# Two transformer blocks at 256 tokens: the first 33 blocks of modulation products moved from DVE to PE

## The reference

```
s_lat, s_ctx = silu(c), silu(c_ctx)
for l in range(2):
    mod   = s_lat @ w_ada[l] + b_ada[l]      # 1024 -> 6 * 1024
    mod_c = s_ctx @ w_ada[l] + b_ada[l]      # same matrix, other vector
    h  = rmsnorm(x,  g1[l]) * (1 + sc1)  + sh1
    hc = rmsnorm(xc, g1[l]) * (1 + csc1) + csh1
    ...
for layer in range(2):                        # type b
    mod = silu(c_2) @ mod_w[layer] + mod_b[layer]   # 1024 -> 9 * 1024
```

## Time and profile before

| | |
|---|---|
| time, median of 3 runs | 2594.62 us (2591.86 to 2596.06) |
| profiled execution: time, span | 2591.45 us, 2589.8 us |
| PE busy, PEld busy | 2318.4 us (90%), 2250.5 us (87%) |
| DVE busy | 1991.8 us (77%) |
| ACT busy | 1254.1 us (48%) |
| mean granted clock of PE | 0.955 |
| HBM traffic | 497 MB read, 192 GB/s |
| modulation products, the group of L865 into `modraw` | 226, mean 1218 ns |
| chain that ended last | PE 67%, DVE 19%, DMA 5%, ACT 4% |

### The profile page before, as it was taken

One profiled execution on the slowest core, in us unless ns is written; L12 is line 12 of the kernel. 1 busy time (PEld: TensorE's weight loads), 2 busy tenths in 40 slices (PEclk: granted clock), 3 DMA queues, 4 the chain that ended last, 5 costly groups with the idle time before them and its releaser, 6 DMA issues.

```text
span 2589.8 us, 49983 instructions
## 1 busy us (share of the span) xinstructions
PE 2318.4 (90%) x18080; PEld 2250.5 (87%) x18080; DVE 1991.8 (77%) x3466; ACT 1254.1 (48%) x1965; POOL 119.9 (5%) x231
## 2 busy tenths in 40 slices
PE   3778699977978999989999999998899999986998
PEld 3767599966878999977999999996899999976998
DVE  7998887969967876896899577668776677687555
ACT  3335266333455654435565454445544544565543
POOL 0000000000000000000000000001000000000000
PEclk9889799988989999989999999998999999998999
DMA  6544555764456555432587667674587587563654
GB/s 252 195 138 153 189 172 180 245 219 133 152 176 203 179 172 185 165 122 90 196 272 262 186 234 261 202 244 156 187 283 242 174 280 252 166 209 95 199 169 135
DMA packets 148461, 500.19 MB, mean 193 GB/s; under 512 B 16480, under 2 KB 17504, under 8 KB 147040
## 3 DMA queue, kind: packets, MB, share of 16 engines
q1 hardware_dynamic: 113472, 375.06, 42.8%
q0 software_dynamic: 32544, 119.03, 15.3%
q10 hardware_dynamic: 2304, 4.20, 0.6%
HBM read 497.16 MB, written 1.05 MB: 192 GB/s over the span
## 4 chain that ended last, share of the span: by engine, by line
PE 67%; DVE 19%; DMA 5%; ACT 4%; issue 4%; DVEq 0%; SPq 0%; POOL 0%; POOLq 0%; ACTq 0%
PE bank_pair L1415 20%; PE bank_pair L1417 20%; PE bank_pair L1416 20%; DVE w_lo L852 4%; DMA modraw<-in_w_mod 4%; DVE arena L1018 3%; DVE modraw L865 2%; DVE x_res L865 2%; PE bank_pair L1590 1%; PE ps_o L1628 1%; PE ps_t L1422 1%; PE ps_t L1601 1%; DVE arena L977 1%; ACT w_hi L494 1%; DVE h_lo L983 1%
## 5 line engine op out<-in xcount | busy, mean ns | idle before, releaser
L852 DVE TENSOR_TENSOR w_lo<-raw,w_hi 128x1024 fp32r<-128x1024 f32 (+3 forms) x772 | 839.9, 1109 | 290.2 <-ACT w_hi L494 287.9
L1415 PE MATMUL bank_pair<-h_hi,w_hi 128*128 128x256 f32 x3344 | 959.6, 287 | 24.6 <-DVE w_lo L852 24.6
L1416 PE MATMUL bank_pair<-h_lo,w_hi 128*128 128x256 f32 x3344 | 952.6, 285 | 0.0
L1417 PE MATMUL bank_pair<-h_hi,w_lo 128*128 128x256 f32 x3344 | 952.3, 285 | 0.0
L494 ACT ACTIVATE w_hi<-raw 128x1024 fp32r<-128x1024 f32 (+3 forms) x772 | 734.3, 964 | 432.9 <-PE bank_pair L1417 327.9
L1415 PEld LDWEIGHTS bank_pair<-h_hi,w_hi 128*128 128x128 f32 x3344 | 648.4, 194 | 36.2 <-DVE w_lo L852 22.5
L1416 PEld LDWEIGHTS bank_pair<-h_lo,w_hi 128*128 128x128 f32 x3344 | 648.7, 194 | 0.2
L1417 PEld LDWEIGHTS bank_pair<-h_hi,w_lo 128*128 128x128 f32 x3344 | 648.3, 194 | 0.0
L1415 PE MATMUL bank_pair<-e_both,w_hi 128*128 128x256 f32 x1774 | 514.7, 290 | 86.5 <-DVE e_both L1369 28.9
L1416 PE MATMUL bank_pair<-e_both,w_hi 128*128 128x256 f32 x1774 | 510.4, 288 | 0.0
L1417 PE MATMUL bank_pair<-e_both,w_lo 128*128 128x256 f32 x1774 | 509.8, 287 | 0.0
(11 more groups left out here) (208 smaller groups left out, 2252.2 us busy)
## 6 DMA issues: line engine op xcount, KB each, us to landing
modraw<-in_w_mod POOLq DMA_DIRECT2D x224, 512.0 KB, 4.6
raw<-in_w_gu SPq DMA_DIRECT2D x176, 512.0 KB, 4.8
raw<-in_w_up SPq DMA_DIRECT2D x132, 512.0 KB, 4.7
raw<-in_w_gate SPq DMA_DIRECT2D x48, 512.0 KB, 4.6
raw<-in_w_dn SPq DMA_DIRECT2D x64, 384.0 KB, 3.6
raw<-in_w_dn SPq DMA_DIRECT2D x64, 320.0 KB, 2.9
raw<-in_w_down SPq DMA_DIRECT2D x48, 384.0 KB, 3.8
raw<-in_w_down SPq DMA_DIRECT2D x48, 320.0 KB, 3.1
```

The source lines that it names most:

```text
L852: nc.vector.tensor_tensor(w_lo[:, p, at], raw[:, p, HALF * f:HALF * f + w], w_hi[:, p, at].bitcast(F32), ALU.subtract).then_inc(lo_ready, 1)
L1415: nc.tensor.matmul(out, l[0], r[0], start=start, stop=False)
L1416: nc.tensor.matmul(out, l[0], r[1], start=False, stop=False)
L1417: return nc.tensor.matmul(out, l[1], r[0], start=False, stop=stop)
```

## The change

The first 33 m-blocks are multiplied on PE. The host lays them out transposed (inputs on the partitions, 128 output columns along the free dimension, for each of eight chunks), and hands over c and c_ctx as a 128 x 8 x 2 tile, `ccol`. For each half, PE makes eight products with the 128 x 128 chunk of the m-block as the stationary operand and two columns, one chunk of both vectors, as the moving one, in plain f32, into four columns of `ps_t` (`pe_mod`); ACT copies the finished four columns into `modcol` (`mod_copy`). There is one such place in PSUM, so half 0 of an m-block waits for the copy of the one before. On PE the products stand at the beginning of a slab, ahead of the slab's own waits; on ACT the copy stands ahead of `prepare`. The m-blocks that the ctx gate stage had are spread over glu, q, k; v, merge, out and down keep theirs. POOL's and SP's loads wait for PE's counter `mod_mm` in place of DVE's. `x_res` is no scratch tile any more, and x and the vector c_2 are loaded at the beginning. The first weight slab is loaded ahead of m-blocks 6 and 7. The norm's first part is reordered: PE does m-blocks 0 and 1 before the sums of squares, 2 to 7 after them, and DVE's shift and scale columns come after its Newton step. m-blocks from 33 on stay on DVE, one vector each.

```diff
-        stage("glu", a[f"w_glu{l}"], SLAB, 2, mods=1)
+        stage("glu", a[f"w_glu{l}"], SLAB, 2, mods=1 + early)
-        stage(qk, a[f"w_q{l}"], SLAB, 1, mods=int(l == 0), arg=dict(...))
-        stage(qk, a[f"w_k{l}"], SLAB, 1, mods=int(early), arg=dict(...))
+        stage(qk, a[f"w_q{l}"], SLAB, 1, mods=2 if early else int(l == 0), arg=dict(...))
+        stage(qk, a[f"w_k{l}"], SLAB, 1, mods=2 * early, arg=dict(...))
-        stage("gate", a[f"w_gate{l}"], SLAB, 4, mods=int(l == 0), arg=dict(l=l, ctx=x == "ctx"))
+        stage("gate", a[f"w_gate{l}"], SLAB, 4, mods=int(l == 0 and not early), arg=dict(l=l, ctx=x == "ctx"))
...
-        unused = res["x"][:, 0:4, :].rearrange("p a b -> p (a b)")
+        ps_mod = ps_t[:, 1, 0:4]
...
 (SP)
+            load(first, 0, 0)
             for k in (6, 7):
-                sp.wait_ge(mod_done, 2 * (k - 5))
+                sp.wait_ge(mod_mm, 2 * (k - 5))
...
-            load(first, 0, 0)
             load(first, 0, 1)
...
 (POOL)
             for c in range(2):
-                load_mod(N_FIRST, c, 2 * 5 + c + 1)
+                load_mod(N_FIRST, c, mod_mm, 2 * 5 + c + 1)
+            nc.gpsimd.dma_start(res["x"][:], a["x"]).then_inc(setup_in[3], 16)
+            nc.gpsimd.dma_start(cact[:, 1, :], a["vectors"][:, D:2 * D]).then_inc(vec_in[2], 16)
...
-            pool.wait_ge(mod_ctx_done, 2 * N_DOUBLE)
-            nc.gpsimd.dma_start(res["x"][:], a["x"]).then_inc(setup_in[3], 16)
...
 (ACT)
+            def mod_copy(m):
+                act.wait_ge(mod_mm, 2 * m + 2)
+                nc.scalar.activation(modcol[:, :, bass.ds(2 * m, 2)], ps_mod.rearrange("p (c v) -> p v c", c=2), ACT.Copy)\
+                    .then_inc(mod_done, 2)
...
 (ACT, do_norm)
+                    if i == 0:
+                        for m in range(2):
+                            mod_copy(m)
                     for k in range(DC):
                         nc.scalar.activation(nsq[:, k, :], x[:, k, :], ACT.Square).then_inc(sq_ready, 1)
...
+                if i == 0:
+                    for m in range(2, N_FIRST):
+                        if m == 6:
+                            split_hi((first, 0, 0), 0)
+                            split_hi((first, 0, 0), 1)
+                        mod_copy(m)
...
 (PE)
+            def pe_mod(m, tile, halves=(0, 1), arrived=None):
+                for c in halves:
+                    if arrived is not None:
+                        pe.wait_ge(mod_in[c], arrived)
+                    if c == 0:
+                        wait_up(pe, mod_done, 2 * m)
+                    for k in range(DC):
+                        ins = nc.tensor.matmul(ps_mod[:, 2 * c:2 * c + 2], tile[:, c, P * k:P * (k + 1)], ccol[:, k, :],
+                                               start=k == 0, stop=k == DC - 1)
+                    ins.then_inc(mod_mm, 1)
...
             def do_slabs(s):
                 def body(b, is_first, last):
                     for p in range(2):
+                        mods(s, b, p)
                         operands_ready(s, b, p, is_first)
...
             def do_norm(n):
+                if n["i"] == 0:
+                    pe.wait_ge(c_ready, 1)
+                    first_mods(range(0, 2))
...
                 ins.then_inc(sum_ready, 1)
+                if n["i"] == 0:
+                    first_mods(range(2, N_FIRST))
```

More of the change, by code:

```diff
@@ L504, in _, with mod_copies @@
             nc.scalar.activation(small[:, 1, :], small[:, 0, :], ACT.Exp, scale=-1.0).then_inc(c_ready, 1)
-            for g, f in ((0, 0), (0, 1), (1, 0)):
-                split_hi((first, 0, g), f)
+            def mod_copy(m):
+                act.wait_ge(mod_mm, 2 * m + 2)
+                nc.scalar.activation(modcol[:, :, bass.ds(2 * m, 2)], ps_mod.rearrange("p (c v) -> p v c", c=2), ACT.Copy)\
+                    .then_inc(mod_done, 2)
+            def mod_copies(s, b, p):
+                if s.m0 < N_DOUBLE:
+                    if s.mods == 2:
+                        mod_copy(s.m0 + 2 * b + p)
+                    if s.mods == 1 and p == 1:
+                        mod_copy(s.m0 + b)
             def do_norm(n):
@@ L540, in do_norm @@
                             .then_inc(hn_hi, 1)
+                if i == 0:
+                    split_hi((first, 0, 1), 0)
                 if n["before"] is not None:
@@ L853, in split_lo @@
                                         ALU.subtract).then_inc(lo_ready, 1)
[L855 to L867, removed]
-            def mods(s, b, p):
[L871 to L875, removed]
+            def mods(s, b, p):
+                if s.m0 < N_DOUBLE:
                     return
@@ L884, in one_mod @@
                 at = m if isinstance(m, int) else m0
-                if at < N_DOUBLE:
-                    columns(m, modraw, 1, 1, False, 16 * (m - N_FIRST + 1), halves)
-                if at >= 2 * N_MOD_A:
-                    dve.wait_ge(c_ready, 4)
-                columns(m, modraw, 0, int(at >= 2 * N_MOD_A), True, 16 * (m - N_FIRST + 1), halves)
+                vec = int(at >= 2 * N_MOD_A)
+                dve.wait_ge(c_ready, 4 if vec else 2)
+                for c in halves:
+                    dve.wait_ge(mod_in[c], 16 * (m - N_FIRST + 1))
+                    nc.vector.scalar_tensor_tensor(out=modraw[:, c, :], in0=modraw[:, c, :], scalar=1.0,
+                                                   in1=cact[:, vec, :], op0=ALU.mult, op1=ALU.mult,
+                                                   accum_out=modcol[:, 0, bass.ds(2 * m + c, 1)]).then_inc(mod_done, 1)
             def pad_edges():
@@ L895, in pad_edges @@
                 link(nc.vector.memset(u_pad[:, :, PAD + T:UW], 0.0))
-            dve.wait_ge(c_ready, 1)
-            for m in range(N_FIRST):
-                dve.wait_ge(first_in[m], 16)
-                columns(m, mod_first[m % 6], 1, 1, False)
-                if m < 2:
-                    dve.wait_ge(c_ready, 2)
-                    columns(m, mod_first[m % 6], 0, 0, True)
             dve.wait_ge(c_ready, 3)
@@ L921, in _ @@
             nc.vector.memset(small[:, 0, :], EPS).then_inc(eps_set, 1)
-            for g, f in ((0, 0), (0, 1), (1, 0)):
-                split_lo((first, 0, g), f)
             def mod_vector(r, v, out, plus):
@@ L955, in do_norm @@
                 i, x, kind = n["i"], res[n["x"]], n["kind"]
-                if not n["fused"]:
+                if not n["fused"] and i > 0:
                     norm_columns(n)
@@ L1417, in mm3, with mods, first_mods @@
                 return nc.tensor.matmul(out, l[1], r[0], start=False, stop=stop)
+            def pe_mod(m, tile, halves=(0, 1), arrived=None):
+                for c in halves:
+                    if arrived is not None:
[6 more added lines that the diff above has]
+                    ins.then_inc(mod_mm, 1)
+            def mods(s, b, p):
+                if s.m0 < N_DOUBLE:
+                    if s.mods == 2:
+                        m = s.m0 + 2 * b + p
+                        pe_mod(m, modraw, (0, 1), 16 * (m - N_FIRST + 1))
+                    if s.mods == 1:
+                        m = s.m0 + b
+                        pe_mod(m, modraw, (p,), 16 * (m - N_FIRST + 1))
+            def first_mods(ms):
+                for m in ms:
+                    pe.wait_ge(first_in[m], 16)
+                    pe_mod(m, mod_first[m % 6])
             def sum_squares(i, k, start, stop):
@@ L1799, in arrays_of @@
                                 + [_pack_rows(i["mod_w_2"][l]) for l in range(2)], 0)
-    vectors = np.concatenate([i["c"][0], i["c_ctx"], i["c_2"][0]])
-    a["vectors"] = np.ascontiguousarray(np.broadcast_to(vectors, (P, 3 * D)))
+    for m in range(N_DOUBLE):
+        w = i["w_ada"][m // N_MOD_A][:, 256 * (m % N_MOD_A):256 * (m % N_MOD_A + 1)]
+        a["w_mod"][m] = w.reshape(DC, P, 2, P).transpose(1, 2, 0, 3).reshape(P, 2 * D)
+    a["vectors"] = np.ascontiguousarray(np.broadcast_to(np.concatenate([i["c"][0], i["c_2"][0]]), (P, 2 * D)))
+    a["vector_cols"] = np.ascontiguousarray(np.stack([_rows(i["c"][0]), _rows(i["c_ctx"])], 2))
     qkv = i["sb_w_qkv_2"][0]
```

43 lines of the change are left out of this document (28 added, 15 removed).

## The result

| | before | after |
|---|---|---|
| median of the runs, us | 2594.61 (2591.86 to 2596.06) | 2637.34 (2634.9 to 2638.85) |
| ratio, 95% interval | | 1.0165 [1.0152, 1.0178] |
| span of the profiled execution, us | 2589.8 | 2633.2 |

The change makes the kernel 1.65% slower, 42.7 us. The span grew by 43.4 us. The forecast was 2651 us, by the case of the cold clock, in a range of 2586 to 2690 us.

What follows compares the result with a forecast made beforehand. DVE was taken to bound q, k and v, PE much of down; after the change, PE. Full-clock terms gave +7.5 us, the cold clock +49: 2591.45 + 56.5 = 2648, then 2651 us on the runs' median; range 2586 to 2690.

Steps and rivals of the forecast that it cites:

- the case of the cold clock: Likeliest case, chance 0.48: weight loads don't count as work for PE's clock, +49 us over full clock, 2651 us.
- Block on PE, 0.11 us per load, 0.21 cold: PE's 32 weight loads per block: 3.5 us at full clock, 3.7 with first latency and wait; 6.8 us cold.
- Full loads: Rival, chance 0.08: PE's loads don't overlap, 0.194 us each, +2.7 us per block, 2686 us.
- the fast step of the 64-column pair: Rival, chance 0.10: loads faster than 0.11 us; at 0.055 us a block takes 1.8 us, 2553 us.
- Start, 22.2 + 17.5: Before the first slab: +22.2 us at full clock; +17.5 for five of blocks 2 to 7 running cold.
- Glu to v, -4.4, with +11.75 and +1 for the clock: Glu, q, k, v stages: 87.6 against 92.0 us at full clock; cold raises a 9.5 us slab to 11.2, v +1.
- Gate, -10 to the convolution's end: Gate stage: blocks leave; five heads give back two DVE products each, 11.5 us, PE allows at least 7.5; 10 taken.
- Last heads, merge and out: Full clock: -2 us for gate's last three heads, -7.7 for merge and out; +2.0 us with the cold surcharge.
- Down, +22.4: Down stage at full clock: PE, already the bound, gets half a block per slab, 93.0 against 70.6 us.
- Down, +7 for the clock: Down stage's cold surcharge: half of the 0.9 us that 27% would cost, +7 us over 16 slabs.
- x start, -13: Start of the x pass: x already in SBUF, squares and warm sums follow at once, 7.9 in place of 20.9 us.
- The rival of the full clock: Chance 0.34: weight loads count as work and the clock stays up, +7.5 us, 2602 us, own range 2588 to 2614.

## Why the prediction was right

The case taken as likeliest is the one that came: the loads at 0.11 us each, and the clock down where the blocks stand. The sum was less exact than its total looks. It gave +56.5 us, and the spans differ by 43.4. Of the 13 us between, 8 are its own terms, which cancel in part: 12.2 us too much for down, 2.8 for the last heads to out and 1.2 for the start, against 4.6 too little for glu to v, 3.2 for the gate and 0.4 for the start of x. The other 5 came back in stages that it had put at nothing.

- **Block on PE, 0.11 us per load, 0.21 cold**: right, 3.63 and 6.96 us. Full loads and the fast step of the 64-column pair are both out.
- **Start, 22.2 + 17.5**: right to 1.2 us, in part by luck. The kernel with 128 columns splits it: 19.1 us (69.94 less 50.82) for the full clock, 3.1 less than my term, and 19.4 for the low one, 1.9 more.
- **Glu to v, -4.4, with +11.75 and +1 for the clock**: 4.6 us too little. A slab took 11.5 us for 11.2, 2.3 us over seven, and the two v slabs with the end of the stage 2.2 more. At full clock I had 9.5 us per slab; the 128-column kernel's slabs lie 9.33 apart (113.08 to 122.41 us).
- **Gate, -10 to the convolution's end**: mis-sized; it was 6.8 on the path. DVE's convolution itself did end 9.3 us earlier in the stage (51.1 us behind the first copy for 60.35), but PE came to its first product with it only 2.5 us later (247.88 us for 245.42). PE is busy 51.83 of 53.6 us in it and as cold as before (0.91 against 0.92), plus 1.8 us of waits. The 7.5 us that I had set as the least, 60.4 less PE's own 52.95, were the most that could come at an unchanged clock, not the least.
- **Last heads, merge and out**: right to 3 us. The 30% of the time at low clock that I took is what 0.85 says for glu to out.
- **Down, +22.4**: mis-sized in what it was compared with. The new length, 93.0 us, came out as 92.5 (500.17 to 592.70 us; 6.10 and 5.38 us per slab for 6.17 and 5.45). But I cut the old stage at 461 us where it begins at 456.95, so 70.6 us should have been 74.7, and the term +18.3.
- **Down, +7 for the clock**: wrong. Half blocks between full slabs left the granted clock at 1.00. I had halved the cost by judgement; it was nothing.
- **x start, -13**: right in size, -12.6; the kernel before with x early gives 3 us less at this place, since its sums are cold; in the change PE works on its half blocks until 1.56 us before them.
- **What took the 5.1 us back** afterwards is not settled. It lies in the second model's stretch from 1688.6 us of before, whose code did not change: 169.5 us there at a granted clock of 0.94, 164.7 us after at 0.98. The clock's drops fall on other places. The kernels with 128 and 64 columns show 166.4 us in it, that with x early 167.6, so every changed kernel is below the one trace of before. I did not test why.

The rival of the full clock comes near with 64 and 128 columns: 2590 and 2586 us for the 2602 I gave it. With 128 columns the trace has the start 3.1 us under that case's terms, glu to out 1.9 and down 5.2 (4.1 of it the wrong cut), the start of x 0.4 over, and 4.1 come back after it. The rule of the Trainium skill that I had weighed (page TensorE: Matmul & The Clock Gate, Part 4: transposes through the array do not count as the multiplications do) is about another kind of work, and no transpose ran here to test it; these thin products behaved in the same sense, with 6.96 us per block at the low clock. That page's figure for products of up to 64 columns (section Back-to-back issue gap), which it gives without the weight load, was no price here, where 0.11 us per load was.

## What to carry to other kernels

A product with few moving columns costs PE its weight loads, and where PE sets the pace a long row of them costs twice: once for itself and once for the slower clock in it and behind it. Read both from the trace before moving such work to PE, and where it must stand there, widen the stream to what hides under the next load. Work is worth moving only out of stages where its engine is the last to finish: here glu to out lost 5.4 us at the low clock and gained 26 at the full one, and down lost 17 to 19 at either width. Compare a new stage with the old one between the same two instructions.

## What the hardware showed that I had not expected

- The granted clock followed the columns streamed behind the loads, at the same loads: in glu to out 0.85 with 2 columns, 0.91 with 32, 0.97 with 64 and 0.98 with 128 (283.3, 270.0, 253.3 and 251.9 us), while PE was busy 97% of that time in all four. A PE that the profile shows as busy can still stand at its low clock.
- The extra columns are nearly free in time: a block takes 3.63 us with 2 and 3.73 with 128.
- A block of 3.63 us between slabs ran at full clock itself; the multiplications behind it ran cold for 3.4 us (111.57 to 114.95 us).
- Half blocks, 1.84 us every 6.1 or 5.4 us, left the clock at 1.00.
